# Router sums formed in token rows by small products; last layer norm with tile 0 added on VectorE and the last store in two halves

## What is computed

```python
out, sc = mix_hgrn2(x, j, lower_bounds[layer], p, s_hgrn[j])
x = layer_norm(ALPHA * x + out, p['ln_c_g'][j], p['ln_c_b'][j])
moe = moe_swiglu(x, p['moe_router'][j], p['moe_w1'][j], p['moe_w3'][j], p['moe_w2'][j])
x = layer_norm(ALPHA * x + moe, p['ln_moe_g'][j], p['ln_moe_b'][j])
# in moe_swiglu:
probs = jax.nn.softmax((x @ router).astype(f32), axis=-1)
top_p, top_e = lax.top_k(probs, TOP_K)
```

## Time and profile before

| | us |
|---|---|
| median of 3 runs | 1533.47 (1531.88 to 1534.13) |
| the profiled execution, its own time | 1532.93 |
| its span, first to last instruction | 1530.9 |
| router, from the first L1077 product to the first L1154 product | 732.1 to 752.5 |
| the end, from the last L1180 product to the last instruction | 1510.0 to 1530.9 |

### The profile page before, as it was taken

One profiled execution on the slowest core, in us unless ns is written; L12 is line 12 of the kernel. 1 busy time (PEld: TensorE's weight loads), 2 busy tenths in 40 slices (PEclk: granted clock), 3 DMA queues, 4 the chain that ended last, 5 costly groups with the idle time before them and its releaser, 6 DMA issues.

```text
span 1530.9 us, 28979 instructions
## 1 busy us (share of the span) xinstructions
PE 1467.2 (96%) x11164; PEld 1309.3 (86%) x11165; DVE 1186.0 (77%) x1610; ACT 943.1 (62%) x1239; POOL 73.5 (5%) x148
## 2 busy tenths in 40 slices
PE   7989999899999899999999999999999999999997
PEld 6978988799999798988878888888888888888884
DVE  5664787754544768877799889998889989899896
ACT  4453135533332478636677778877787777877873
POOL 8200000000000000000000000000000000000000
PEclk9989999899999999999999999999999999999999
DMA  8411003244444343221899999999999999999992
GB/s 249 159 56 66 4 4 124 84 160 143 153 136 152 111 150 113 92 78 46 326 357 404 397 388 398 367 382 399 345 398 361 391 398 342 398 359 400 396 340 85
DMA packets 162031, 371.71 MB, mean 243 GB/s; under 512 B 10152, under 2 KB 85840, under 8 KB 161936
## 3 DMA queue, kind: packets, MB, share of 16 engines
q1 hardware_dynamic: 159408, 361.19, 64.0%
q0 software_dynamic: 2160, 7.87, 1.9%
q10 hardware_dynamic: 368, 1.31, 0.2%
HBM read 360.63 MB, written 9.71 MB: 242 GB/s over the span
## 4 chain that ended last, share of the span: by engine, by line
PE 86%; DVE 8%; ACT 3%; issue 2%; DMA 0%; SPq 0%; DVEq 0%; ACTq 0%
PE bank L1154 10%; PE bank L1155 10%; PE bank L1156 10%; PE bank L529 9%; PE bank L530 9%; PE bank L531 9%; PE bank L1178 5%; PE bank L1180 5%; PE bank L1179 5%; PE bank L621 4%; PE bank L1163 1%; PE bank L934 1%; DVE wd_lo L1250 1%; ACT wd_hi L2165 1%; PE bank L983 1%
## 5 line engine op out<-in xcount | busy, mean ns | idle before, releaser
L1915 DVE TENSOR_TENSOR w_lo<-moe_ring,w_hi 128x1024 fp32r<-128x1024 f32 (+1 forms) x560 | 608.5, 1157 | 29.7 <-ACT w_hi L2613 29.7
L2613 ACT ACTIVATE w_hi<-moe_ring 128x1024 fp32r<-128x1024 f32 (+1 forms) x560 | 531.4, 1014 | 72.8 <-PE bank L1180 39.1
L1250 DVE TENSOR_TENSOR wd_lo<-arena,wd_hi 128x1024 fp32r<-128x1024 f32 x142 | 170.6, 1208 | 166.7 <-ACT wd_hi L2165 166.3
L529 PE MATMUL bank<-in_hi,wd_hi 128*128 128x320 f32 x880 | 279.5, 318 | 20.5 <-DVE in_lo L1616 14.0
L1154 PE MATMUL bank<-w_hi,xe_hi 128*128 128x512 f32 (+1 forms) x768 | 288.2, 375 | 1.3 <-DVE w_lo L1915 1.3
L1155 PE MATMUL bank<-w_hi,xe_lo 128*128 128x512 f32 (+1 forms) x768 | 285.9, 372 | 0.0
L1156 PE MATMUL bank<-w_lo,xe_hi 128*128 128x512 f32 (+1 forms) x768 | 285.4, 372 | 0.0
L530 PE MATMUL bank<-in_lo,wd_hi 128*128 128x320 f32 x880 | 275.3, 313 | 0.0
L531 PE MATMUL bank<-in_hi,wd_lo 128*128 128x320 f32 x880 | 275.1, 313 | 0.0
L2165 ACT ACTIVATE wd_hi<-arena 128x1024 fp32r<-128x1024 f32 x142 | 147.7, 1046 | 174.8 <-PE bank L531 166.2
L529 PEld LDWEIGHTS bank<-in_hi,wd_hi 128*128 128x128 f32 x880 | 168.6, 192 | 24.9 <-issue 17.8
(11 more groups left out here) (405 smaller groups left out, 1716.6 us busy)
## 6 DMA issues: line engine op xcount, KB each, us to landing
moe_ring<-in_moe_w SPq DMA_DIRECT2D x216, 1024.0 KB, 8.8
moe_ring<-in_moe_w SPq DMA_DIRECT2D x64, 768.0 KB, 5.5
arena<-in_ffn_w SPq DMA_DIRECT2D x30, 1024.0 KB, 5.1
arena<-in_w_in_c SPq DMA_DIRECT2D x16, 1024.0 KB, 5.3
arena<-in_w_in_ab SPq DMA_DIRECT2D x13, 1024.0 KB, 5.1
arena<-in_w_out_ab SPq DMA_DIRECT2D x4, 1024.0 KB, 5.0
arena<-in_w_out_c SPq DMA_DIRECT2D x4, 1024.0 KB, 4.8
arena<-in_ffn_w SPq DMA_DIRECT2D x4, 768.0 KB, 4.2
```

Of the source, the lines that this page charges most:

```text
L529: pe.matmul(b[:, 0:T], w_[0][:, cols], x_hi, start=start, stop=False)
L1250: dve.tensor_tensor(wd_lo[:, m_ % DENSE_UNITS, 0:words], src, wd_hi[:, m_ % DENSE_UNITS, 0:words], ALU.subtract).then_inc(S("dense_lo"), 1)
L1915: dve.tensor_tensor(w_lo[:, i % UNITS, 0:unit_words(i)], moe_unit(i), w_hi[:, i % UNITS, 0:unit_words(i)], ALU.subtract)\
L2613: act.activation(w_hi[:, i % UNITS, 0:unit_words(i)], moe_unit(i), ACT.Copy).then_inc(S("e_hi"), 1)
```

## The change

In the router the operands change places: the tokens are now the stationary operand (128, 128 and 64 columns of `res` or the squares), and the 10 useful columns of `logit_w` the moving one. So the sums arrive in token rows at once. The 11 products become 33 and one more, with zeros, that fills the unused rows of the third tile. ACT's copy to `stats`, DVE's memset of its unused columns and the three turning products go, and all 24 transposes of the residual now follow the sums. SP's wait for `c_ln_full` becomes one for the finished sums.

In the last norm tile 0 is no longer added by PE: DVE adds the rows loaded back to the product in PSUM (two halves, result in `xtok`), takes the moments there and subtracts the mean in one instruction of 1024 columns. For tiles 1 and 2 PE still adds, half by half. The last tile's final step and its store are cut into two halves.

```diff
             order = [("res", k) for k in range(KC - 2)] + [("sq", 0), ("res", KC - 2), ("sq", KC - 2), ("res", KC - 1), ("sq", KC - 1)]
-            for i, (kind, k) in enumerate(order):
-                half = slice(64 * (i % 2), 64 * (i % 2) + C)
+            for o, (kind, k) in enumerate(order):
                 if kind == "res":
                     pe.wait_ge(*(at_count("c_centered", k + 1) if k < EARLY_K else at_count("c_res", k + 1)))
-                    w, x = logit_w[:, NL + k * NL:NL + k * NL + C], res[:, k, :]
+                    w, x = logit_rows[:, k, :], res
                 else:
                     pe.wait_ge(*(at_count("c_sq", k + 1) if k else at_count("c_scaled", 2)))
-                    w, x = logit_w[:, 0:C], sq[:, k, :]
-                mm = pe.matmul(b[half, 0:T], w, x, start=i < 2, stop=i >= len(order) - 2)
-                if i >= len(order) - 2:
-                    mm.then_inc(S("c_ln_full"), 1)
+                    w, x = logit_w[:, 0:NL], sq
+                for i, (t0, n) in enumerate(TILES):
+                    mm = pe.matmul(b[0:n, i * NL:(i + 1) * NL], x[:, k, t0:t0 + n], w, start=(o == 0 and i == 0),
+                                   stop=(o == len(order) - 1), skip_group_check=True)
+                if o == 0:
+                    pe.matmul(b[64:P, 2 * NL:3 * NL], ones[:, 0:64], logit_w[:, LOGIT_W - NL:LOGIT_W], start=False, stop=True,
+                              skip_group_check=True)
+            mm.then_inc(S("logit_full"), 1)
...
-            rows_turned(0, 0)
-            b = take(("logit", 1), "logits_done", 2)
-            pe.wait_ge(*at_count("logits_done", 1))
-            pe.wait_ge(*at_count("router_ready", 3))
             for i in range(3):
-                mm = pe.matmul(b[:, i * NL:(i + 1) * NL], stats[:, i * P:(i + 1) * P], ident2[:, 0:NL], start=True, stop=True)
-            mm.then_inc(S("logit_full"), 1)
-            rows_turned(0, 1)
-            for i in (1, 2):
                 for h in range(2):
                     rows_turned(i, h)
...
-            act.wait_ge(*at_count("c_ln_full", 3))
-            act.activation(stats[:, 0:T], where["logit", 0][:, 0:T], ACT.Copy).then_inc(S("logits_done"), 1)
...
-                        sp.wait_ge(*at_count("c_ln_full", 3))
+                        sp.wait_ge(*at_count("logit_full", 1))
...
+                pe.wait_ge(*at_count("y_scale", 1))
                 for i, (t0, rows) in enumerate(TILES):
-                    pe.wait_ge(*at_count(f"y_in{i}", 16))
+                    if i:
+                        pe.wait_ge(*at_count(f"y_in{i}", 16))
                     for half in range(2):
-                        pe.matmul((E_H1, E_H3, E_T)[i][half][0:rows, :], ident[:, 0:rows], xtok[:, i, half * 512:(half + 1) * 512],
-                                  start=True, stop=False)
-                    if i == 0:
-                        pe.wait_ge(*at_count("y_scale", 1))
-                    for half in range(2):
-                        if i == 0:
+                        if i:
+                            pe.matmul((E_H1, E_H3, E_T)[i][half][0:rows, :], ident[:, 0:rows], xtok[:, i, half * 512:(half + 1) * 512],
+                                      start=True, stop=False)
+                        else:
                             pe.wait_ge(S("e_y"), 2 * n - 1 + half)
...
+            dve.wait_ge(*at_count("y_in0", 16))
             dve.wait_ge(*at_count("ln_gb_in", 64))
             for i, (t0, n) in enumerate(TILES):
                 for h in range(2):
                     dve.wait_ge(*at_count("y_normal", 2 * i + h + 1))
-                    dve.bn_stats(moments[0:n, i, h, :], (E_H1, E_H3, E_T)[i][h][0:n, :]).then_inc(S("y_moments"), 1)
+                    x = (E_H1, E_H3, E_T)[i][h][0:n, :]
+                    if i == 0:
+                        cols = slice(h * 512, (h + 1) * 512)
+                        link(dve.tensor_tensor(xtok[:, 0, cols], xtok[:, 0, cols], x, ALU.add))
+                        x = xtok[:, 0, cols]
+                    dve.bn_stats(moments[0:n, i, h, :], x).then_inc(S("y_moments"), 1)
...
-            for i in range(3):
+            for i in range(2):
                 sp.wait_ge(*at_count("y_done", i + 1))
-                dst = outs[0][0][i * P:(i + 1) * P, :] if i < 2 else outs[1][0]
-                sp.dma_start(dst, xtok[0:TILES[i][1], i, :]).then_inc(S("stored"), 16)
-            sp.wait_ge(*at_count("stored", 16 * (2 + 2 + 3)))
+                sp.dma_start(outs[0][0][i * P:(i + 1) * P, :], xtok[:, i, :]).then_inc(S("stored"), 16)
+            for h in range(2):
+                sp.wait_ge(*at_count("y_done", 3 + h))
+                sp.dma_start(outs[1][0][:, h * 512:(h + 1) * 512], xtok[0:T_SAMPLE, 2, h * 512:(h + 1) * 512]).then_inc(S("stored"), 16)
+            sp.wait_ge(*at_count("stored", 16 * (2 + 2 + 4)))
```

More of the change, by code:

```diff
@@ L362, in mixed_trunk @@
         router_b = rt[:, 0:3].rearrange("p a i n -> p (a i n)")[:, 0:KC * NE].rearrange("p (k n) -> p k n", k=KC)
-        stats = xT.rearrange("p k t -> p (k t)")[:, 0:3 * P]
         res_flat = arena[:, NORM0:NORM0 + KC * T + T]
@@ L1111, in _ @@
             pe.wait_ge(*at_count("xtok_done", 6))
-            pe.wait_ge(*at_count("logits_done", 2))
+            pe.wait_ge(*at_count("logits_done", 1))
             def unit(n, i):
@@ L1218, in last_rows @@
             def last_rows(n):
+                pe.wait_ge(*at_count("y_scale", 1))
                 for i, (t0, rows) in enumerate(TILES):
-                    pe.wait_ge(*at_count(f"y_in{i}", 16))
+                    if i:
+                        pe.wait_ge(*at_count(f"y_in{i}", 16))
                     for half in range(2):
-                        pe.matmul((E_H1, E_H3, E_T)[i][half][0:rows, :], ident[:, 0:rows], xtok[:, i, half * 512:(half + 1) * 512],
-                                  start=True, stop=False)
-                    if i == 0:
-                        pe.wait_ge(*at_count("y_scale", 1))
-                    for half in range(2):
-                        if i == 0:
+                        if i:
+                            pe.matmul((E_H1, E_H3, E_T)[i][half][0:rows, :], ident[:, 0:rows], xtok[:, i, half * 512:(half + 1) * 512],
+                                      start=True, stop=False)
+                        else:
                             pe.wait_ge(S("e_y"), 2 * n - 1 + half)
                         pe.matmul((E_H1, E_H3, E_T)[i][half][0:rows, :], pick[:, i, 0:rows], ey[:, half * 512:(half + 1) * 512],
-                                  start=False, stop=True).then_inc(S("y_normal"), 1)
+                                  start=(i == 0), stop=True).then_inc(S("y_normal"), 1)
             expert_loops(pe, expert_block, last_rows)
@@ L1916, in weight_rest @@
                    .then_inc(S("e_lo"), 1)
-            dve.wait_ge(*at_count("c_res", KC))
-            dve.memset(stats[:, T:3 * P], 0.0).then_inc(S("router_ready"), 1)
             dve.memset(pos[:, NE, :], -1e6)
@@ L1923, in _ @@
                 weight_rest(0, i)
-            landed = where["logit", 1][:, 0:3 * NL].rearrange("p (i n) -> p i n", n=NL)
+            landed = where["logit", 0][:, 0:3 * NL].rearrange("p (i n) -> p i n", n=NL)
             dve.wait_ge(*at_count("logit_full", 1))
@@ L1934, in _ @@
                .then_inc(S("c_scaled"), 1)
-            dve.wait_ge(*at_count("logits_done", 2))
+            dve.wait_ge(*at_count("logits_done", 1))
             link(dve.tensor_tensor(lg[:, :, :], lg[:, :, :], bc(router_sum[:, 1, :], 1, 3), ALU.add))
@@ L2112, in _, with halves @@
             expert_loops(dve, expert_block, last_places)
+            def halves(i):
+                if i == 0:
+                    return [(slice(0, D), xtok[:, 0, :])]
+                return [(slice(h * 512, (h + 1) * 512), (E_H1, E_H3, E_T)[i][h][0:TILES[i][1], :]) for h in range(2)]
             def centred(i):
@@ L2117, in centred @@
                 dve.wait_ge(*at_count("y_var", i + 1))
-                for h in range(2):
-                    cols = slice(h * 512, (h + 1) * 512)
-                    ins_ = dve.scalar_tensor_tensor(xtok[0:n, i, cols], (E_H1, E_H3, E_T)[i][h][0:n, :], mean_var[0:n, i, 0:1], ln_gb[0:n, 0, cols], ALU.subtract, ALU.mult)
+                for cols, x in halves(i):
+                    ins_ = dve.scalar_tensor_tensor(xtok[0:n, i, cols], x, mean_var[0:n, i, 0:1], ln_gb[0:n, 0, cols], ALU.subtract, ALU.mult)
                 ins_.then_inc(S("y_scaled"), 1)
@@ L2127, in scaled @@
                 dve.wait_ge(*at_count("y_scaled", i + 1))
-                dve.scalar_tensor_tensor(xtok[0:n, i, :], xtok[0:n, i, :], rstd[0:n, i, 0:1], ln_gb[0:n, 1, :], ALU.mult, ALU.add)\
-                   .then_inc(S("y_done"), 1)
+                for cols in [slice(0, D)] if i < 2 else [slice(0, 512), slice(512, D)]:
+                    dve.scalar_tensor_tensor(xtok[0:n, i, cols], xtok[0:n, i, cols], rstd[0:n, i, 0:1], ln_gb[0:n, 1, cols],
```

(2 more changed lines are left out.)

## The result

The changed kernel takes 1537.53 us (median of 7 runs, 1536.04 to 1538.6) and the one before 1533.43 (7 runs, 1530.95 to 1534.37): the ratio is 1.003, 95% interval 1.002 to 1.004. It is slower by 4.1 us, which is more than measurements of this kernel scatter. The profiled execution took 1538.03 and has a span of 1536.2, 5.3 longer than before.

A forecast was written before the change was run, and what follows sets the result against it. PE was taken to bound the router sums, then DVE the choice of experts, in series. Sums 3.8, fallen clock 4.1, transposes and position products 0.8, less 1.9 at the end, gave +6.8 us, about 1540; range 1532.5 to 1542.

The forecast's parts named there:

- the forecast's own band: Whole kernel: the range of times given to the main forecast itself, 1538.5 to 1541.5 us, with chance 0.50.
- rival B: Router sums: no price for switching width, but the clock falls; +2.9 us, 1536.4; chance 0.09.
- The price of a group: Router sums: three products in six passes, paced by weight loads and width switches, take 0.76 us at the upper clock.
- The clock: Router sums: PE's clock falls to the lower level some 4.0 us after 732.09 (3.2 to 5.0).
- Rival A: Router sums: the clock holds since PE never idles; +1.9 us, 1535.4, or 1533.0 if the later fall vanishes; chance 0.25.
- C: Router sums: no price for switching width and the clock holds; -0.2 us, 1533.3; chance 0.05.
- What the fallen clock costs in the sums: Router sums: the remaining 4.6 us take 1.9 times as long, a group 1.43; 4.1 us more.
- Transposes and position products, +0.8: Behind the sums: slower transposes cost 0.7 and position passes 0.6, taken as 0.8 together; gather L1213 left unchanged.
- SP's wait: Router: gain, bias and next weight loads start some 5 us later, covered by pieces in the ring; cost nothing.
- The end: Last norm: 1.2 us from the addition, 0.1 from mean and gain together, 0.6 from the store; 1.9 gained.
- Rival E: Last norm: the idle gap stands ahead of tile 0's products; forecast plus 2, 1542; chance 0.06.
- Rival D: Router: no switching price, clock holds, fall before the gather gone; 1530.9, needing a group below 0.56 us; chance 0.05.

The follow-up runs named there:

- by_tile: Changed kernel with the sums of the two full tiles first, the third tile's behind them; 1534.69 us, ratio 1.0007 to the kernel before.
- cols64: Changed kernel with 64 moving columns instead of 10 in each router product; 1534.92 us, ratio 1.0013 to the kernel before.
- by_tile_cols64: Changed kernel with full tiles first, third tile behind, and 64 moving columns; 1531.33 us, ratio 0.9992 to the kernel before.
- rows_held: by_tile_cols64 plus nine products that serve nothing, seven before the position products, two before the gather; 1531.95 us, ratio 0.999 to the kernel before.
- router_only: Kernel before with only the router sums changed to token rows, last norm as before; 1539.38 us, ratio 1.0037 to the kernel before.
- store_only: Kernel before with only the last norm's final step and last store cut in halves; 1532.85 us in one run.

## Why the prediction was right, and where a term was off

**Sign and size.** Measured are 1537.53 us and +4.1 by the medians, +4.64 by the two stretches that the change touches; the forecast was 1540 and +6.8, the range 1532.5 to 1542. The sign was right, and so were the steps that carry most of it: loads that set the pace, a price for the change of width, and a clock that falls while PE is busy. The sum was 2.1 us too high: three terms were too large by 0.3, 1.0 and 0.9, and the end's gain by 0.1 the other way. The median thus lies 1 us below the forecast's own band and nearer to the 1536.4 of rival B than to 1540; what speaks for the forecast's mechanism is the measured price of a group, not the time.

**The price of a group** (0.76 us) measured 0.757, with all its parts: 0.11, 0.21, 0.06, 0.16. They came from rows of other stages with the same widths. That the change of width costs something is shown by `by_tile`, 8.6 us of sums for 11.4. The eleven groups together are a little less than I summed: the first, with the products of zeros, took only 0.66, and 0.66 + 10 x 0.757 = 8.2, with the end 8.3, not 8.6: +3.5, not +3.8.

**The clock** fell 3.6 us into the sums, forecast 4.0 (3.2 to 5.0), with PE never idle. `cols64` shows why: with more columns in the same passes it stays up. The Trainium skill (TensorE: Matmul & The Clock Gate, "Why this matters for your kernels") has it that the full clock is kept when no long idle gaps stand between bursts; 13.50 us of 13.50 busy at PEclk 0.50 speak against that, and the measurement decides. Rival A fell with it, and B and C with the price of a group. One of the prediction's grounds was weaker than it reads: that the program's start ran at the lower level follows from the length of the records alone, since the trace has no granted clock on record before 18.70.

**What the fallen clock costs in the sums** was mis-sized: a group took 1.27, 1.7 times the upper price, and not 1.43, 1.9 times. The step that failed is "where the switches are my estimate at the lower clock": the steps put at 0.40, 0.11 and 0.29 measured 0.36, 0.06 and 0.26, and one of the three at 0.21 measured 0.17. Six groups at 0.52 more are 3.1 us (11.4 - 8.3), not 4.1. Nearly half of the error lies here.

**Transposes and position products, +0.8.** The transposes took 5.38 us (forecast 5.3), and PE was 0.5 late for the choice (749.20, with DVE's `rt` there at 748.65; forecast 0.7). The position passes lost little, since the clock rose in the midst of them, at 749.9. But the term was wrong as a whole, by the step "L1213 I leave as it was": the gather took 7.22 us for 8.06. It met the lower clock from 753.3 to 756.7, 3.4 us, where it had met it for 5.1, from 744.0 to 749.1: about 16 passes at 0.21 instead of 24, 0.8 us less. From the end of the sums to the first expert product it is 15.46 us for 15.55 before: -0.1, not +0.8. It is not the early fall that makes the later one shorter: in `cols64` and `by_tile_cols64` there is no early fall, and the clock is down in the gather for 3.4 us all the same (749.5 to 753.0, 744.5 to 747.9), with 7.22 us for it. All five kernels with sums in token rows and no added products have this, and `rows_held`, too, is down for 3.4. What in the new router does it is open.

**SP's wait** cost nothing: the expert stage lasts 757.18 for 757.17.

**The end** gained 1.79 where 1.9 was forecast, and in the parts named: 1.15 (1.2) up to the aggregate, 0.13 (0.1), the store 0.52 net (0.6, in which the 0.14 lost by cutting the last step in two was not counted). It was right partly by luck: the 1.2 holds against an execution with the gap of 0.65 in it; where the gap is absent for another reason, the addition is worth 0.5 to 0.9. Rival E, the gap ahead of tile 0's products, didn't come: their 0.78 of idle time ended with ACT's `ey`.

**The sum by measured terms:** 3.5 + 3.1 - 0.1 - 1.8 = +4.7, against +4.64 in the stretches. Rival D, the other side, needed a group below 0.56 us; even `by_tile_cols64` stands at 0.58 (6.4 / 11), and its router was longer than before's by 0.7 us.

## What to carry to other kernels

When operands change places so that the few useful columns are the moving ones, count weight loads and not columns: with loads of 0.11 us in front of 10 columns, 66 passes took longer than 22 passes of 320 columns. Order the products so that the stationary width seldom changes, and look at the granted clock wherever PE moves little in a pass, even if it is never idle. Where the clock falls just ahead of a stretch of real work, products that serve nothing, put into time in which PE waits anyway, can be worth as much (1.8 us here) as an edit of the arithmetic; whether they hold the clock must be seen in the trace, since in one of two kernels they didn't.

## What the runs showed of the hardware that was not expected

- A pass with more moving columns can end sooner in sum: 66 passes of 64 columns took 9.2 us, the same passes of 10 columns 11.4, since the latter lost the clock.
- A change of the stationary width between 128 and 64 columns costs 0.10 us each way at the upper clock (0.21 for 0.11, 0.16 for 0.06), 0.28 us for both with 64 moving columns (`cols64` less `by_tile_cols64`, 2.84 for ten pairs).
- In the changed kernel the clock came back at 749.9, half a microsecond behind 24 transposes that ran at the lower level without idle time, and fell again at 753.3, 1.4 us into a gather without idle time; 0.97 us of idle time and the small position products had stood ahead of it. In the kernels whose sums kept the clock up, it fell inside the gather too.
- 0.65 us of idle time with no releaser stood in the kernel before and was absent in `router_only` and `store_only`, where PE's instructions around it were the same. What sets it is open.
